# Reordering scores, top-slot transposes, the first weighted split and the retention means in a fused two-block transformer kernel

## What is computed

```python
def head_groupnorm(o, g):
    mu = jnp.mean(of, axis=-1, keepdims=True)
    var = jnp.mean((of - mu) ** 2, axis=-1, keepdims=True)
    y = (of - mu) * lax.rsqrt(var + EPS)
...
def peer_ffn(h, w_pq, sub_keys, expert_u, expert_v):
    q = (h @ w_pq).reshape(B, S, PEER_HEADS, 2, PEER_DQ // 2)
    scores = jnp.einsum('bshpd,hpkd->bshpk', q, sub_keys)
    top_s, top_i = lax.top_k(scores, K)              # 16 of 128, twice per head
    cand_s = top_s[..., 0, :, None] + top_s[..., 1, None, :]
    best_s, best_pos = lax.top_k(cand_s, K)          # 16 of 256
    gate = jax.nn.softmax(best_s, axis=-1)
    a = jnp.einsum('cd,chkd->chk', hc, u)            # chosen rows of expert_u
    w = gc * jax.nn.gelu(a, approximate=False)
    return jnp.einsum('chk,chkd->cd', w, v)          # chosen rows of expert_v
```

## Time and profile before

| what | us |
|---|---|
| median of three executions | 2905.5 |
| lowest and highest of the three | 2903.01 and 2906.28 |
| the profiled execution, its own time | 2902.05 |
| its span in the trace | 2900.3 |

### The profile page before, as it was taken

One profiled execution on the slowest core, in us unless ns is written; L12 is line 12 of the kernel. 1 busy time (PEld: TensorE's weight loads), 2 busy tenths in 40 slices (PEclk: granted clock), 3 DMA queues, 4 the chain that ended last, 5 costly groups with the idle time before them and its releaser, 6 DMA issues. The chain is left out here.

```text
span 2900.3 us, 40006 instructions
## 1 busy us (share of the span) xinstructions
PE 2791.4 (96%) x16468; PEld 2382.6 (82%) x16468; DVE 2090.9 (72%) x3086; ACT 1408.0 (49%) x1620; POOL 192.0 (7%) x168
## 2 busy tenths in 40 slices
PE   6989999999999999999999999998999999999998
PEld 6768888788888788888878888887888888888887
DVE  6777866665543669989879955435599989699755
ACT  4554445554456445554444444484445544444443
POOL 0200001000003001110000000030011200000000
PEclk9989999999999999999999999999999999999999
DMA  8747854545543355554445555533445544455554
GB/s 320 288 174 272 311 206 168 202 167 192 192 180 131 117 174 175 189 174 162 173 160 189 175 189 195 217 126 121 157 163 189 189 160 163 158 192 174 186 193 148
DMA packets 75637, 537.41 MB, mean 185 GB/s; under 512 B 8512, under 2 KB 8896, under 8 KB 12096
## 3 DMA queue, kind: packets, MB, share of 16 engines
q1 hardware_dynamic: 75456, 534.86, 52.7%
HBM read 527.48 MB, written 7.34 MB: 184 GB/s over the span
## 5 line engine op out<-in xcount | busy, mean ns | idle before, releaser
L946 ACT ACTIVATE whi<-raw 128x2048 fp32r<-128x2048 f32 x438 | 838.6, 1915 | 985.9 <-issue 827.6
L1396 DVE TENSOR_TENSOR wlo<-raw,whi 128x2048 fp32r<-128x2048 f32 x438 | 1006.3, 2298 | 331.0 <-ACT whi L946 330.3
L428 PE MATMUL banks<-ht,whi 128*128 128x512 f32 x3136 | 771.5, 395 | 7.4 <-DVE big L1470 5.4
L428 PEld LDWEIGHTS banks<-ht,whi 128*128 128x128 f32 x3136 | 576.5, 189 | 123.3 <-issue 6.9
L503 PE MATMUL banks<-whi,ht 128*128 128x512 f32 x1152 | 459.6, 399 | 18.2 <-DVE ht L1460 10.0
L505 PE MATMUL banks<-whi,ht 128*128 128x512 f32 x1152 | 452.7, 393 | 0.0
L436 PEld LDWEIGHTS banks<-ht,wlo 128*128 128x128 f32 x3136 | 401.9, 191 | 15.8
L436 PE MATMUL banks<-ht,wlo 128*128 128x256 f32 x3136 | 406.6, 283 | 0.0
L513 PE MATMUL banks<-wlo,ht 128*128 128x512 f32 x1152 | 287.4, 389 | 0.0
L503 PEld LDWEIGHTS banks<-whi,ht 128*128 128x128 f32 x1152 | 218.6, 190 | 65.3 <-issue 19.3
L505 PEld LDWEIGHTS banks<-whi,ht 128*128 128x128 f32 x1152 | 218.7, 190 | 44.3
(11 more groups left out here) (259 smaller groups left out, 3263.6 us busy)
## 6 DMA issues: line engine op xcount, KB each, us to landing
raw<-in_pu SPq DMA_DIRECT2D x128, 1024.0 KB, 4.9
raw<-in_pv SPq DMA_DIRECT2D x128, 1024.0 KB, 4.9
raw<-in_win SPq DMA_DIRECT2D x52, 1024.0 KB, 4.9
big<-in_wmod SPq DMA_DIRECT2D x24, 1024.0 KB, 6.4
raw<-in_wmod SPq DMA_DIRECT2D x24, 1024.0 KB, 4.9
raw<-in_wgate SPq DMA_DIRECT2D x22, 1024.0 KB, 4.9
raw<-in_wup SPq DMA_DIRECT2D x22, 1024.0 KB, 4.9
raw<-in_wdown SPq DMA_DIRECT2D x22, 1024.0 KB, 4.9
```

The source lines that it names most:

```text
L428: m = e.matmul(bank[b + n], h[:, q, c[n]], M.both[:, q * 512:(q + 1) * 512], start=q == 0, stop=False, skip_group_check=True)
L946: e.activation(whi(j), slot[u][0], ACT.Copy).then_inc(*hi.mark(j))
L1396: e.tensor_tensor(wlo(j), slot[u][0], whi(j).bitcast(F32), ALU.subtract).then_inc(*lo.mark(j))
```

## The change

The diff has four parts. (A) In the loop over nine pq steps, the ninth step now computes expert unit a0 before the scores of head 7, on PE, ACT and DVE; the loops of expert units start at 1. On DVE that takes one `some(2.4)` away. (B) The transposes of the slots go to banks 0 and 1 instead of two banks of the turn 4 to 7, and the gate plan starts at unit 33 with `pace` shifted by one. (C) On ACT the split of w0 is put ahead of the copy of a63, and the split of w1 ahead of its gelu; on DVE `split_weights(0)` is put ahead of `activated(63)`. (D) ACT no longer copies banks 2 and 3; DVE sums straight from the banks, before its parts of the first output transposes, and subtracts from the banks into `os`, and only then makes the next `wlo`.

```diff
     def pace(u):
-        return 2 if u % 4 == 0 else 1
+        return 2 if u % 4 == 1 else 1
...
             for i in range(9):
-                if i < 8:
-                    wide_unit(("pq", l, i), HT, ready)
+                wide_unit(("pq", l, i) if i < 8 else ("a", l, 0), HT, ready)
...
                 if u == GATES:
                     for t in range(2):
-                        b = clear(("top", l, t))
+                        b = clear(("top", l, t), t)
...
-                due = plan.step(pace(u))[0] if GATES <= u < 58 else []
+                due = plan.step(pace(u))[0] if GATES < u < 58 else []
...
-                wide_unit(("a", l, u), HT, ready, between)
+                if u:
+                    wide_unit(("a", l, u), HT, ready, between)
...
             upto(used[0] + 1)
-            for t in range(2):
-                key = ("ov", l, 2 + t)
-                on.wait_ge(*valued.at(("ret", l, 3)))
-                e.copy(os[t][:, 512:1024], psum(key)[:, :]).then_inc(*took_a.mark(key))
             head_squares(("o2", l, 1), [o[:, 512:1024] for o in os], sqs,
-                         lambda t: on.wait_ge(*normal.at(("o2", l, "mean", t))))
+                         lambda t: on.wait_ge(*took_v.at(("ov", l, 2 + t))))
...
+            for u in range(1, 64):
+                if u == GATES - 1:
+                    exponent()
+                k = take()
+                upto(k + 2)
+                gelu(u - 1)
+                if u == 63:
+                    mm1 = k
+                    split_weights(0)
+                region(on, l, u)
+                apart(ag(u * 512, 512), ("a", l, u), k)
+            split_weights(1)
+            gelu(63)
...
-            out_parts(("o2", l), l, (0, 1))
-            upto(used[0] + 1)
+            raw = [psum(("ov", l, 2 + t))[:, :].rearrange("p (n d) -> p n d", n=4) for t in range(2)]
+            on.wait_ge(*valued.at(("ret", l, 3)))
             for t in range(2):
-                on.wait_ge(*took_a.at(("ov", l, 2 + t)))
-                e.tensor_reduce(mu[:, t * 4:t * 4 + 4], ov[t], X, ALU.add).then_inc(*normal.mark(("o2", l, "sum")))
+                e.tensor_reduce(mu[:, t * 4:t * 4 + 4], raw[t], X, ALU.add).then_inc(*normal.mark(("o2", l, "sum")))
+            out_parts(("o2", l), l, (0, 1))
...
-                e.tensor_tensor(ov[t], ov[t], mu[:, t * 4:t * 4 + 4].unsqueeze(2).broadcast_to([P, 4, 128]),
-                                ALU.subtract).then_inc(*normal.mark(("o2", l, "mean", t)))
+                e.tensor_tensor(ov[t], raw[t], mu[:, t * 4:t * 4 + 4].unsqueeze(2).broadcast_to([P, 4, 128]),
+                                ALU.subtract).then_inc(*took_v.mark(("ov", l, 2 + t)))
+            upto(used[0] + 1)
...
             for i in range(9):
-                if i < 8:
-                    take()
+                take()
...
-            for u in range(64):
+            for u in range(1, 64):
...
-            activated(63)
-
...
             split_weights(0)
+            activated(63)
```

More of the change, by code:

```diff
@@ L1321, in peer @@
             for i in range(9):
+                k = take()
+                since()
                 if i < 8:
-                    k = take()
-                    since()
                     apart(ag(QT + i * 512, 512), ("pq", l, i), k)
+                else:
+                    region(on, l, 0)
+                    apart(ag(0, 512), ("a", l, 0), k)
                 if i:
@@ L1330, in peer @@
                     e.copy(ag(SC + (i - 1) * 512, 512), psum(key)[:, :]).then_inc(*took_a.mark(key))
-            def gelu(u):
-                x = ag(u * 512, 512)
-                on.wait_ge(*took_v.at(("a", l, u)))
-                e.activation(x, x, ACT.Gelu).then_inc(*a_soft.mark(("gelu", l, u)))
-            for u in range(64):
-                if u == GATES - 1:
-                    exponent()
-                k = take()
-                upto(k + 2)
-                if u:
-                    gelu(u - 1)
-                region(on, l, u)
-                apart(ag(u * 512, 512), ("a", l, u), k)
-            gelu(63)
-            mm1 = k
             def split_weights(v):
@@ L1353, in split_weights, with gelu @@
                     split(HT.hi[:, (v % 2) * 2:(v % 2) * 2 + 2], ag(v * 512, 512), ("w", l, v))
-            split_weights(0)
+            def gelu(u):
+                x = ag(u * 512, 512)
+                on.wait_ge(*took_v.at(("a", l, u)))
+                e.activation(x, x, ACT.Gelu).then_inc(*a_soft.mark(("gelu", l, u)))
+            for u in range(1, 64):
+                if u == GATES - 1:
+                    exponent()
+                k = take()
+                upto(k + 2)
[7 more added lines that the diff above has]
+            gelu(63)
             for v in range(64):
                 k = take()
-                split_weights(v + 1)
+                if v:
+                    split_weights(v + 1)
             last_h[0] = k
@@ L2043, in peer @@
                 take()
-                if u:
-                    activated(u - 1)
+                activated(u - 1)
                 if u == GATES - 2:
@@ L2053, in peer @@
                     slots_turned(l, 1)
-                if GATES <= u < 58:
+                if GATES < u < 58:
                     gate_step(l, 0, *plan.step(pace(u)))
```

## The result

| | before | after |
|---|---|---|
| median of the runs made side by side, us | 2904.26 (4 runs, 2902.06 to 2906.28) | 2877.28 (4 runs, 2874.1 to 2879.48) |
| the profiled execution, its own time | 2902.05 | 2876.52 |
| its span | 2900.3 | 2874.8 |

The ratio is 0.9909, 95% interval 0.9895 to 0.9922: 27 us faster. The forecast was 2879.0 in a range of 2871 to 2889.

What follows compares the result with a forecast made beforehand. PE, busy 2791 of 2900 us, was taken as the bound, so only its idle time and slow matmuls could be won: 17.2 idle plus 9.6 clock, 26.8 off the median 2905.5, gives 2879, range 2871 to 2889.

Steps and rivals of the forecast that it cites:

- the sum: Whole kernel: idle time 17.2 plus clock 9.6, together 26.8 us won.
- Idle time: PE's waits at the four parts, both layers: A 5.6, B 4.8, C 3.7, D 3.1, together 17.2 us won.
- the chain of the queries: Part A: head 7's queries ready at 1104.2, PE waits 0.0 to 0.2, 3.2 us won before a deduction.
- a2 named as late next: Part A: unit a2 waits for DVE's join of a0; 0.35 us (0 to 1.0) taken off per layer.
- The prediction's doubt by the rule of the ports: Part B: by the shared-port rule alone only POOL, not L1396, would be lengthened; two losses of 0.3 us would vanish.
- The gates ahead of unit 58: Part B's later plan: second one-hot ready at 6.4, needed at 6.6; cost 0 (0 to 0.3 us a layer).
- Clock: Slow matmuls behind the gaps: A 1.5, B 3.4, C 3.0, D 3.4, together 11.3 us, of which 9.6 counted.
- I leave one loss of 1.7 of the four: Gaps left at C (2.0) and D (1.5), both layers: one clock loss of 1.7 us assumed to remain.
- The 1.5 of part A: Second layer, behind the last scores' gap: 16 high matmuls at 5.41 against 3.91, 1.5 us of clock won.
- Rival 1: Only idle time is won; clock losses move to gaps keeping their place (C, D, norms): 2888 us, chance 0.14.
- Rival 2: Output projection: DVE's low halves still delay L1460, so part D's 3.1 and 3.4 are missing: 2885.5 us, chance 0.11.
- Rival 3: Units a1 to a30: DVE's turn becomes the bound and the kernel gets slower, 2916 us, chance 0.03.

Runs made afterwards that it cites:

- bud25: The changed kernel with DVE's selection budget raised from 2.4 to 2.5 per unit; 2873.49 us, ratio 0.9895 to before.
- no_a: The changed kernel with part A alone undone (scores of head 7 again ahead of unit a0); 2877.83 us, ratio 0.9919 to before.
- b_fill: The kernel before with 19 unused 128-column matmuls behind the slot transposes; 2903.11 us, ratio 0.9996 to before.
- b_fill11: The kernel before with 11 unused 128-column matmuls behind the slot transposes; 2897.96 us, ratio 0.9983 to before.
- again: The changed kernel run once more, unaltered; 2876.61 us, ratio 0.9911 to before.
- bud34: The changed kernel with DVE's selection budget raised from 2.4 to 3.4 per unit; 2907.86 us, ratio 1.0023 to before.
- fillc: The changed kernel with 14 unused 128-column matmuls in the gap before the first weighted unit; 2872.48 us, ratio 0.9889 to before.
- no_d: The changed kernel with part D alone undone (ACT copies banks 2 and 3, DVE sums from the copy); 2884.67 us, ratio 0.9935 to before.
- no_b: The changed kernel with part B alone undone (slot transposes in banks 4 to 7, gate plan from unit 32); 2882.24 us, ratio 0.9928.

## Why the prediction was right, and where it was off

The time (2877.3 for 2879.0) and the sum (25.5 by the profile, 27.0 by the medians, for 26.8) came out, and the parts can be held against the forecast one by one.

**Idle time** was forecast at 17.2 and measured at 17.1. Part A: the chain of the queries, and a2 named as late next, are what the trace shows; the wait there is 0.17, where I took off 0.35. Part B: 2.68 gone, 0.34 come, for 0.3, and `bud25` and `no_a` show that the moved budget is the cause. The prediction's doubt by the rule of the ports rested on a misreading, as said at part B above; its number did not. The gates ahead of unit 58 cost nothing: no wait for L1992 or L1993 is in the list. Part C: 1.85 for 1.84. Part D: 1.06 and 0.49 as forecast. The sums from banks took 1.29 for two, so 0.65 each, no more than from SBUF.

**Clock** was forecast at 9.6 kept; 8.7 was. The weak step is "I leave one loss of 1.7 of the four": the gaps at C and D are not four of a kind. The two of 1.50 at D kept the clock in every variant. The two of 2.00 at C both lost it. D gave more than its 3.4 (3.9), and C nothing of its 3.0, where 1.7 had been allowed for; what is left of the difference is small because of that allowance. The better rule from the rows that I had would have been to ask of each gap left over how long it is, and to count the 2.00 like the 1.99 of the earlier trace rows, which had lost clock in the kernel before, rather than to place it between 1.50 and 2.68. This row was in my own list. The 1.5 of part A depends on the profile that it was read from: the scores' gap of 2.99 lost clock once of two times in the profile of before, but twice in `b_fill`, twice in `b_fill11` and never in `no_a`.

**Rival 1** said that losses would move to gaps that keep their place. These profiles show no such move. Behind 930, outside the four stretches and up to the last 6 us, the half-clock time is 17.1, 13.7 and 10.2 in the profiles of before, `b_fill` and `b_fill11`, and 13.7 both in after and in `again`. The 3.0 near 872 and the 1.4 near 1040 were not in the sum; they vary from execution to execution of the same program (see the ledger), and what decides them stays open: the row ahead of the first, an idle time of 1.18, is the same with and without the loss. So that the time came out within 2 us is in part luck, since such differences alone had moved one program's arrival at L734 by up to 9.5 from profile to profile.

**Rival 2** fell: D's chain ended 0.4 earlier than I had reckoned, the low half (L1396) behind it runs from 952.22 to 954.50, and the rounded parts come from ACT only at 954.06 to 955.6. L1460 waits 0.43 for ACT, and no longer for DVE's own low half. **Rival 3** is real and was rightly made unlikely; `bud34` puts its threshold between 2.5 and 3.4 of budget.

The chance of faster (0.95) rested on all cases but one winning over 15. The four undone parts bear this out, since each of them leaves the kernel 17 or more under before.

## What to carry to other kernels

On an engine that is 96% busy, list its idle gaps, and price each as the gap plus the slow matmuls behind it: at B the 2.68 was 62% of the cost, at the norms all that could be won was the second term. Undoing one part and comparing times can mislead where clock falls elsewhere (`no_a`: 2.9 us by the times, within their noise, and 5.7 in its own stretch); measure the stretch from marker to marker as well. Where a wait can't be removed, unused matmuls in the gap can keep the clock, and what they overrun the gap by is taken off the gain (nothing in `b_fill11`, part of it in `fillc`, nearly all in `b_fill`). And before a difference of a few us between two profiles is put down to an edit, look whether it arose ahead of the edit.

## What the runs showed of the hardware

- **Gap and clock.** At the gaps of this study (length, then half clock behind it or not): 1.50 at D and 1.54 at C, kept each time; 1.99 at D, behind a gap of 1.06 and short transposes, lost in 8 of 8 (`before`, `no_d`, `b_fill`, `b_fill11`); 2.00 at C, lost in 11 of 14 (the changed kernel, `again`, `no_b`, `no_d`, `bud25`, `bud34`; kept twice in `no_a` and once in `bud34`); 2.10 and 2.68 at B, lost in 4 of 4; 2.99 at the scores, kept three times and lost five (`before`, `no_a`, `b_fill`, `b_fill11`); 3.02 at five of the norms, lost in 45 of 65, and 4.3 at the sixth, in 13 of 13; 3.85 at C, lost in 8 of 8. So a longer gap isn't always the one that pays, and the same gap in the same program may or may not. A loss costs 1.4 to 1.7 on a 512-column unit.
- **fp32 matmuls of 128 columns** are recorded as two passes of 0.11 (x28 for 14), and 12 of them fill 2.8.
- **DVE and POOL** hold each other up for the rest of a whole instruction, both ways: DVE 2.29 became 2.86, and POOL's multiplication, 0.7 at its shortest, took 2.78.
- **Reading a bank is no dearer than reading SBUF** for DVE's sums: 1.29 for two, against 1.27.
